# Two attention steps between the gate's matmuls in place of one

## The reference

```python
s = jnp.einsum('bhqd,bhkd->bhqk', qb, k).astype(jnp.float32) * scale
...
s = jnp.where(allowed, s, NEG_INF)
p = jax.nn.softmax(s, axis=-1).astype(v.dtype)
return jnp.einsum('bhqk,bhkd->bhqd', p, v)
...
gates = jax.nn.sigmoid(h @ w_gate[i] + b_gate[i])
merged = ga * (ya @ w_branch_a[i]) + gb * (yb @ w_branch_b[i]) + gc * (yc @ w_branch_c[i])
x = x + rms_norm(merged @ w_out[i], g_mix_post[i])
```

## Time and profile before

| | |
|---|---|
| median of 3 runs | 2093.56 us (2093.19 to 2094.24) |
| the profiled execution | 2093.33 us, its span 2091.3 us |
| TensorE busy | 2009.2 us, 96% of the span |
| DVE busy | 1131.8 us, 54% |
| ACT busy | 783.3 us, 37% |
| POOL busy | 122.6 us, 6% |
| mean granted TensorE clock | 0.981 of full |

### The profile page before, as it was taken

The page is one execution under the profiler, slowest core; times in us unless marked ns, Lnnn a source line. Parts: engine busy times, 40 slices in busy tenths (PEclk is TensorE's granted clock), DMA queues, the critical chain, the costliest instruction groups (busy, mean ns, idle before and its releaser), DMA issues. The chain is left out here.

```text
span 2091.3 us, 26428 instructions
## 1 busy us (share of the span) xinstructions
PE 2009.2 (96%) x9541; PEld 1622.4 (78%) x9541; DVE 1131.8 (54%) x1983; ACT 783.3 (37%) x1359; POOL 122.6 (6%) x91
## 2 busy tenths in 40 slices
PE   8999998899999999999989999978999999999997
PEld 6777776677878888888867777757788788888886
DVE  5444446544566767525674444464445677774266
ACT  4243431343344444314433434314433344443152
POOL 0000000001100111000000000100001011010000
PEclk9999999899999999999999999989999999999999
DMA  5411132112422333332343111321124233333321
GB/s 156 106 33 41 53 85 75 40 51 61 162 81 84 97 100 93 98 121 91 86 126 81 31 51 51 91 61 51 41 78 154 81 91 100 99 92 111 104 88 71
DMA packets 256436, 176.06 MB, mean 84 GB/s; under 512 B 52148, under 2 KB 240464, under 8 KB 256080
## 3 DMA queue, kind: packets, MB, share of 16 engines
q1 hardware_dynamic: 256200, 174.56, 28.5%
q10 hardware_dynamic: 136, 0.16, 0.1%
HBM read 170.31 MB, written 4.36 MB: 84 GB/s over the span
## 5 line engine op out<-in xcount | busy, mean ns | idle before, releaser
L592 PE MATMUL psum<-xnh,wh 128*128 128x512 f32 (+1 forms) x1408 | 569.0, 404 | 10.0 <-DVE vB L1409 6.3
L592 PE MATMUL psum<-xnh,wl 128*128 128x512 f32 (+1 forms) x1408 | 552.4, 392 | 0.0
L592 PE MATMUL psum<-xnl,wh 128*128 128x512 f32 (+1 forms) x1408 | 551.6, 392 | 0.0
L1251 DVE TENSOR_TENSOR wl<-raw,wh 128x1024 fp32r<-128x1024 f32 (+1 forms) x276 | 364.0, 1319 | 327.2 <-ACT wh L1007 326.6
L1007 ACT ACTIVATE wh<-raw 128x1024 fp32r<-128x1024 f32 (+1 forms) x276 | 291.6, 1056 | 527.0 <-PE psum L592 518.6
L592 PEld LDWEIGHTS psum<-xnh,wh 128*128 128x128 f32 (+1 forms) x1408 | 265.8, 189 | 68.0 <-issue 17.4
L592 PEld LDWEIGHTS psum<-xnh,wl 128*128 128x128 f32 (+1 forms) x1408 | 264.8, 188 | 58.8 <-issue 0.2
L592 PEld LDWEIGHTS psum<-xnl,wh 128*128 128x128 f32 (+1 forms) x1408 | 266.0, 189 | 49.7 <-issue 0.2
L1366 DVE TENSOR_REDUCE mx<-psum 128x1 f32<-128x128 f32 (+3 forms) x128 | 62.6, 489 | 163.0 <-PE psum L743 145.4
L1061 ACT ACTIVATE Pr<-psum,nm 128x128 f32<-128x128 f32 (+3 forms) x128 | 67.7, 529 | 207.4 <-DVE nm L1367 207.4
L592 PE MATMUL psum<-wh,fh 128*128 128x512 f32 x288 | 112.0, 389 | 0.0
(11 more groups left out here) (235 smaller groups left out, 3023.8 us busy)
## 6 DMA issues: line engine op xcount, KB each, us to landing
raw<-in_w_up_dram SPq DMA_DIRECT2D x88, 512.0 KB, 3.7
raw<-in_w_gate_dram SPq DMA_DIRECT2D x48, 512.0 KB, 3.6
raw<-in_w_down_dram SPq DMA_DIRECT2D x44, 512.0 KB, 3.5
raw<-in_w_in_dram SPq DMA_DIRECT2D x40, 512.0 KB, 3.7
raw<-in_w_out_dram SPq DMA_DIRECT2D x16, 512.0 KB, 3.6
raw<-in_w_ple_gate_dram SPq DMA_DIRECT2D x16, 512.0 KB, 4.3
raw<-in_w_in_dram SPq DMA_DIRECT2D x16, 256.0 KB, 3.3
raw<-in_w_branch_a_dram SPq DMA_DIRECT2D x8, 512.0 KB, 3.3
```

The source lines that it names most:

```text
L592: ins = pe.matmul(out, left, right, start=start and n == 0, stop=stop and n == 2)
L1251: dve.tensor_tensor(low[:, 0:n], raw[(L * NCH + c) % RAW][:, 0:n], hi[:, 0:n].bitcast(F32), ALU.subtract).then_inc(w_lo.sem, 1)
```

## The change

The attention goes by groups g = 0 to 19 in place of steps. Group g does, on TensorE, score(2g) and score(2g + 1), then turn(2g - 2) and turn(2g - 1), then product(2g - 4) and product(2g - 3), and in groups 6, 10, 14 and 18 the turn of `ytok`. DVE does both maxima, then `ytok` in groups 5, 9, 13, 17, and L1389 in groups 7, 11, 15, 19. ACT does both exponentials, then both copies, then the copy of the turned `ytok`. The 20 groups are spread over the same places: g x 48 // 20 in A, g x 96 // 20 in C and B. The semaphores, buffers, banks and their turn-taking, and every instruction's operands are the same. Cut to its core:

```diff
-ATT_STEPS = STEPS + 6
+GROUPS = STEPS // 2 + 4
+def pair(n):
+    return [s for s in (n, n + 1) if 0 <= s < STEPS]
 def transpose_banks():
     out, n = {}, 0
-    for s in range(ATT_STEPS):
-        if 2 <= s <= STEPS + 1:
-            out[("pt", s - 2)] = n % 2
+    for g in range(GROUPS):
+        for u in pair(2 * g - 2):
+            out[("pt", u)] = n % 2
             n += 1
-        if s >= 5 and (s - 5) % H == H - 1:
-            out[("y", (s - 5) // H)] = n % 2
+        if g >= 6 and g % 4 == 2:
+            out[("y", (g - 6) // 4)] = n % 2
             n += 1
...
     places = n_chunks * KT
-    out = [s for s in range(ATT_STEPS)
-           if (s * places // ATT_STEPS) // KT == local and (k is None or (s * places // ATT_STEPS) % KT == k)]
+    out = [g for g in range(GROUPS)
+           if (g * places // GROUPS) // KT == local and (k is None or (g * places // GROUPS) % KT == k)]
...
# TensorE
-            if s < STEPS:
+            for s in pair(2 * g):
...
-            if 2 <= s <= STEPS + 1:
-                u = s - 2
+            for u in pair(2 * g - 2):
...
-            if 3 <= s <= STEPS + 2:
-                u = s - 3
+            for u in pair(2 * g - 4):
...
-            if s >= 5 and (s - 5) % H == H - 1:
-                i = (s - 5) // H
+            if g >= 6 and g % 4 == 2:
+                i = (g - 6) // 4
...
# ACT: the exponentials by pair(2 * g), the copies by pair(2 * g - 2), ytok as on TensorE
# DVE
-            if s < STEPS:
+            for s in pair(2 * g):
...
-            if s >= 4 and (s - 4) % H == H - 1:
-                i = (s - 4) // H
+            if g >= 5 and g % 4 == 1:
+                i = (g - 5) // 4
...
-            if s >= 6 and (s - 6) % H == H - 1:
-                i = (s - 6) // H
+            if g >= 7 and g % 4 == 3:
+                i = (g - 7) // 4
```

More of the change, by code:

```diff
@@ L155, with att_groups @@
 UP_LINKS = 6
+def pair(n):
+    return [s for s in (n, n + 1) if 0 <= s < STEPS]
 def transpose_banks():
     out, n = {}, 0
-    for s in range(ATT_STEPS):
-        if 2 <= s <= STEPS + 1:
-            out[("pt", s - 2)] = n % 2
+    for g in range(GROUPS):
+        for u in pair(2 * g - 2):
+            out[("pt", u)] = n % 2
             n += 1
-        if s >= 5 and (s - 5) % H == H - 1:
-            out[("y", (s - 5) // H)] = n % 2
+        if g >= 6 and g % 4 == 2:
+            out[("y", (g - 6) // 4)] = n % 2
             n += 1
     return out
-def att_steps(n_chunks, local, k=None):
+def att_groups(n_chunks, local, k=None):
     places = n_chunks * KT
-    out = [s for s in range(ATT_STEPS)
-           if (s * places // ATT_STEPS) // KT == local and (k is None or (s * places // ATT_STEPS) % KT == k)]
+    out = [g for g in range(GROUPS)
+           if (g * places // GROUPS) // KT == local and (k is None or (g * places // GROUPS) % KT == k)]
     return out
@@ L709, in _, with attention @@
         taken = {}
-        def attention(L, a, s):
+        def attention(L, a, g):
             n = STEPS * a
@@ L715, in nk @@
                 return P * (i + 1) if a != 1 else (P if i == 0 else 192)
-            if s == 0:
+            if g == 0:
                 first = {0: ST_A, 1: ST_A + 6, 2: ST_B}[a]
@@ L799, in between @@
                 if att is not None:
-                    for s in att_steps(att[2], c - att[1], k):
-                        attention(L, att[0], s)
+                    for g in att_groups(att[2], c - att[1], k):
+                        attention(L, att[0], g)
             def g_open(j):
@@ L1145, in slot @@
             if att is not None:
-                for s in att_steps(att[2], c - att[1]):
-                    attention(L, att[0], s)
+                for g in att_groups(att[2], c - att[1]):
+                    attention(L, att[0], g)
         act.wait_ge(const_in, 64)
```

## The result

The changed kernel takes 2144.02 us (median of 4 runs, 2140.28 to 2147.49) against 2093.38 (2092.86 to 2094.24): a ratio of 1.0243, 95% interval 1.0228 to 1.0258. It is slower, as forecast, and 17 us above the 2127 predicted: inside the range of 2103 to 2147, outside the 2111 to 2140 that the forecast gave for its own mechanism. The profiled execution took 2147.49 us, with a span of 2145.5 against 2091.3. In the changed kernel's lines, L597 is the dense matmul (L592 before), L747, L748 and L751 the scores and the mask (L742, L743, L746), L760 the turn (L756), L771 the product (L768), L780 the turn of `ytok` (L777), L1064 the exponential, L1075 ACT's copy, L1391 the subtraction (L1389).

A forecast was written before the change was run, and what follows sets the result against it. TensorE, busy 96% of the span, was taken as the bound. 2093.3 us + 51 new waits - 12 old waits - 10 for fewer changes + 5 clock = 2127.3; 2111 to 2140 for this mechanism, 8-in-10 range 2103 to 2147.

The forecast's parts named there:

- The waits for L1391: In attention, a group's second turn waits for `ytok`'s bank, freed by DVE only after both maxima: 16.8 us a layer.
- the walk: Instruction-by-instruction timing of a group: a turn waits 1.3 to 1.5 us in mid-slot, 1.7 to 2.7 at slot starts.
- The waits of `ytok`'s turn: In groups 6, 10 and 14, `ytok`'s turn waits for ACT's copy behind two exponentials: 8.0 us a layer.
- The waits that go: Attention's present waits of TensorE, for copies, L1389 and a branch's bank, counted as gone: 12 us.
- The clock: Half-rate stretches behind TensorE's waits: three more than now, 5 us; none to ten gives 0 to 17.
- rival (c): The clock falls after most of the waits, ten or more stretches: 2142 to 2155 us, chance 0.08.
- The changes: Fewer changes between attention and gate matmuls on TensorE, 20 interruptions for 38: 5 us a layer, 10 in all, saved.
- The return to the gate: The first gate matmul after attention costs 0.08 us extra; saving 18 gives 1.4 us in each of A, B and C.
- going out: Going from gate matmul to score costs nothing in A and B, 0.09 us in C: 1.4 us saved there.
- The second score behind a mask: Inside a pair, the second score follows the first's mask matmul: taken as 0, at most 6 us for 64 pairs.
- Rival (a): The new waits are hidden, under 22 us, and only the gain is left: 2071 us, chance 0.06.

The follow-up runs named there:

- e1: The changed kernel with DVE's low-half subtraction of `ytok` (L1391) moved ahead of both maxima of its group; 2096.06 us.
- e5: The changed kernel with every group two places later in its stage, off the starts of slots; 2120.12 us.
- e2: The changed kernel with TensorE turning `ytok` one place, three gate matmuls, behind its group; 2130.56 us.
- e6: The changed kernel with DVE making the low-half subtraction of `ytok` twice, the second giving the semaphore; 2172.19 us.
- e7: The changed kernel with the subtraction ahead of the maxima, `ytok` turned one place later and every group two places later; 2068.97 us.

## Why the prediction was right, and what was off

**The waits for L1391: right in place, number and size.** Forecast 18 waits, 33.6 us from start to start, 1.4 in mid-slot and 1.7 to 2.7 at slot starts; found 18 waits, 31.5 us idle, the longest 2.5. The two parts of the walk, DVE's own order and its lateness at the start of a slot, are shown apart by e1 and e5 (24 us and 7).

**The waits of `ytok`'s turn: right in kind.** Forecast 16 us with 18 waits, found 12.8 with 16. e2 takes all but 3.3 away by giving ACT the time of three matmuls.

**The waits that go: one row was not looked at.** The forecast took 12 us from the rows on copies, L1389 and the branch. Those it named are gone. It missed the 5.6 us of the last block's `ytok` turn in C and B, which also are gone; the likely reason is that five places now lie between the division and that turn, where there were two. In place of them 1.8 us are new, stage C's first pair waiting for its exponentials; the forecast had such a wait, 0.6 us, in stage A, where none is found. In idle time the waits changed by 33.1 us; the forecast had 51 - 12 = 39.

**The clock: the term that was mis-sized.** The forecast took three more half-rate stretches, 5 us, between 0 and 17. Found: 12 stretches more, many of them of 6.8 us, 58 us in all, which cost 29. It had seen two equal waits of 1.4 us, of which one was followed by such a stretch, and then gave the 18 turn waits and the 18 smaller ones a far smaller share than that one in two; ten of the 18 turn waits had a stretch, so the row's own share was the better estimate. Its upper bound of ten stretches was a number without a row. e6 and e1 show by more and by less waiting that the stretches come with these waits. The forecast's rival (c) is this case: 2142 to 2155 us, held at 0.08, for what came out as 2144. That the total is only 17 us off is in part luck: the waits were 6 us too large (39 against 33), the clock 24 too small. The rule of the Trainium skill that was weighed there (TensorE: Matmul & The Clock Gate, section HAM oscillation — how this bites in real kernels), that it is the long idle gaps which cost clock, would have made the term 0; the trace disagrees, with stretches at 0.50 behind waits of 2.5 us and less.

**The changes: right in sum by luck, wrong in their parts.** Forecast 10 us, found 10 in the changed kernel and 13 in e7, but nearly all of it is stage C. TensorE's busy time less half of its half-rate time goes there from 107.9 us a stage to 102.6 and 102.2 in the changed kernel, 5.5 against the forecast 2.8. In A it stays (88.3 and 88.5 before, 88.7 and 88.5 after; 87.2 and 87.1 in e7, which no run explains), and in B too (114.5 and 114.4 before, 114.9 in both layers after). The forecast had 1.4 less in each.

The return to the gate costs what it said, and 16 of them are saved in a stage, 1.3 us. Against it stand 16 more products behind a product (0.112 start to start) in place of a gate matmul behind a product (0.084), 0.4 us, and the second score behind a mask, 0.8 us, which is shown below. In A and B the three cancel. In C, going out costs the 0.09 of the earlier trace rows for half as many interruptions, 1.5 us saved, and the second score of a pair is cheap, some 3 us that the forecast did not have:

```profile
224.57 0.39 PE L597 MATMUL psum<-y0h,wl 128*128 128x512 f32 x1
224.89 0.92 PE L751 MATMUL psum<-kC,qC 64*128 64x192 f32 x4
225.74 0.66 PE L760 MATMUL psum<-cst,Pr 128*128 128x128 f32 x4
```

This is e7's timeline in stage C. Two scores take 0.85 us (224.89 to 225.74) where one took 0.52 in the earlier trace rows (251.73 to 252.25); from start to start the four matmuls take 0.27, 0.16, 0.16 and 0.25.

**The second score behind a mask: its start right, its price at nothing wrong.** In the changed kernel's stage A:

```profile
159.92 1.02 PE L747 MATMUL psum<-kA,qA 65*128 65x512 f32 x2
...
160.78 0.22 PE L748 MATMUL psum<-cbf 128*128 128x128 bf16 x1
...
160.84 1.07 PE L747 MATMUL psum<-kA,qA 65*128 65x512 f32 x2
...
161.75 0.22 PE L748 MATMUL psum<-cbf 128*128 128x128 bf16 x1
```

It follows at 0.06 us, as the turn does in the earlier trace rows; all 64 such places have a median of 0.059. But the forecast took the start for the price. The first score, behind a gate matmul, has its mask 0.86 us later (159.92 to 160.78), the second, behind a mask, 0.91 us later (160.84 to 161.75). A score is recorded as two matmuls, and it is the first of them that takes longer, in A and in B alike (medians): with four key blocks 0.48 us to its successor behind a mask against 0.43 behind a gate matmul, with three 0.38 against 0.33, with two 0.27 against 0.22. For 64 pairs it is some 3 us, a term that the sum had at 0. The turn could not show it, since a turn takes 0.11 us in any place. The Trainium skill's page TensorE: Matmul & The Clock Gate (section LDWEIGHTS (loading the stationary operand)) gives a weight load as columns / 1.2 ns, an estimate of 0.107 us for 128 columns, of which the mask's 0.06 would cover half. Here the trace agrees with it, in the 0.05 us and in the 3 us of the whole.

**Rival (a)**, waits hidden, needed new waits under 22 us. The changed kernel had 46 at attention. With the three edits of e7 the rival's case was as good as made true (4.7 us of such waits), and the time came out at 2069 where (a) had said 2071.

## What to carry to other kernels

Before steps are put together, follow each buffer that is handed out in turn to the instruction that gives it back, and ask where that instruction stands in its own engine's order relative to what the same group must do: here the bank's release stood behind two maxima of the group whose second turn needed it. Price a wait of TensorE by more than its length where its clock has been seen to fall behind one: here a us of wait was worth nearly 2. And place work off the moments at which another engine is known to be busy, here the first two places of a slot, once the order itself is right.

## What the runs showed of the hardware

Waits of 2.5 us and less, about six in a stage of 97 to 134 us, took the granted clock of busy stretches to 0.50 for 3.4 or 6.8 us at a time: 75 us in all against 17, and 110 when each wait was 0.75 us longer. Waits of at most 1.7 us (e1, 22.3 us of them in all) left the half-rate time at 17; waits of up to 1.6 us, but 33.5 us of them (e5), gave 39. In the changed kernel a wait of 2.19 us kept the clock and one of 1.22 was followed by 0.50. What decides between the two is not settled by these runs; the changed kernel's and e5's times also spread over 7 and 14 us from run to run, where the kernel before spreads over 1.4 (four runs) to 7 (twenty).

Scores with 64 rows of weights (stage C) have an entry price of 0.1 us, behind a gate matmul. For 192 columns the first matmul of a run of them takes 0.27 us to its successor and the last 0.25, and those in the middle of a run of four 0.16.

A score with 65 or 96 rows of weights takes 0.05 us more to its successor when it stands behind a 128-column bf16 matmul, 0.06 us behind its start, than behind a 512-column one (medians at the full clock, with two to four key blocks).
